# Low parts of the natural weight pieces: formed by accumulating DMAs on GpSimd instead of a subtraction on VectorE

## The reference

```python
S, D = 512, 1024
xn = rms(x, norm_w)                                   # layer 1
h = xn @ w_in                                         # 1024 x 4096
qa, ka, va, ga, qr, kr, vr, gr = split(h)
oa = diff_attention(rms(qa), rms(ka), va, lam)        # 4 heads, two softmaxes each
orr = bidirectional_retention(qr, kr, vr, decays)     # 4 heads, chunks of 128
x = x + concat(rms(oa) * silu(ga), orr * silu(gr)) @ w_out

h = rms_norm(x, norm_g_2)                             # layer 2
v_c, b_c, c_c, z_c, q, k, v, z_a, gates = split(h @ w_in_2)     # 1024 x 8704
y_a = (b_c * causal_conv(c_c * v_c) * silu(z_c)) @ w_conv_out_2
y_b = (sliding_window_attention(rms(q), rms(k), v, sinks) * silu(z_a)) @ w_attn_out_2
g_a, g_b = split(sigmoid(gates + gate_b_2))
out = x + (g_a * y_a + g_b * y_b) @ w_out_2
```

## Time and profile before

| | |
|---|---|
| median of 3 runs | 842.09 us (842.07 to 842.28) |
| profiled execution, its own time | 841.2 us |
| its span in the profile | 839.4 us |
| PE busy | 832.9 us, 3998 matmuls |
| DVE busy | 530.3 us; of it the subtraction L823 158.8 us in 128 |
| ACT busy | 254.9 us |
| POOL busy | 181.1 us; of it the rounding L508 143.9 us in 128 |
| DMA | 74.26 MB, packets 28.9% of 16 engines' span |
| granted clock of PE | 1.00 throughout |

### The profile page before, as it was taken

One profiled execution on the slowest core, in us unless ns is written; L12 is line 12 of the kernel. 1 busy time (PEld: TensorE's weight loads), 2 busy tenths in 40 slices (PEclk: granted clock), 3 DMA queues, 4 the chain that ended last, 5 costly groups with the idle time before them and its releaser, 6 DMA issues.

```text
span 839.4 us, 10665 instructions
## 1 busy us (share of the span) xinstructions
PE 832.9 (99%) x3998; PEld 689.1 (82%) x3998; DVE 530.3 (63%) x1005; ACT 254.9 (30%) x603; POOL 181.1 (22%) x194
## 2 busy tenths in 40 slices
PE   9999999999999999999999999999999999999998
PEld 7787888888888888888888888888888888888886
DVE  4898778868973485785577978796642222444421
ACT  4364465642212234433454455430000000000000
POOL 3121111011111111111223434442211212111210
PEclk9999999999999999999999999999999999999999
DMA  6222211121152322232232222222333333333231
GB/s 234 84 93 85 67 51 51 51 76 51 50 201 76 101 76 76 75 101 76 79 89 80 75 73 75 75 82 80 101 101 101 86 90 101 101 99 90 87 127 73
DMA packets 101225, 74.26 MB, mean 88 GB/s; under 512 B 3325, under 2 KB 87350, under 8 KB 101174
## 3 DMA queue, kind: packets, MB, share of 16 engines
q1 hardware_dynamic: 100614, 71.48, 27.9%
q10 hardware_dynamic: 560, 2.11, 0.7%
HBM read 71.48 MB, written 2.10 MB: 88 GB/s over the span
## 4 chain that ended last, share of the span: by engine, by line
PE 91%; DVE 3%; ACT 2%; SPq 2%; issue 1%; POOL 1%; DMA 1%; ACTq 0%; DVEq 0%; POOLq 0%
PE proj L1231 26%; PE proj L1229 26%; PE proj L1230 26%; PE bank_t L1243 3%; PE bank_o L1315 2%; PE score L1301 1%; PE score L1300 1%; PE score L1390 1%; PE score L1389 1%; DMA w_raw<-in_w_in_dram 1%; PE bank_o L1408 1%; PE score L1277 1%; PE bank_o L1409 1%; ACT mix_hi L703 1%; SPq L453 1%
## 5 line engine op out<-in xcount | busy, mean ns | idle before, releaser
L823 DVE TENSOR_TENSOR w_lo<-w_raw,w_hi 128x1024 fp32r<-128x1024 f32 x128 | 158.8, 1242 | 179.1 <-POOL w_hi L508 178.4
L508 POOL TENSOR_SCALAR w_hi<-w_raw 128x1024 fp32r<-128x1024 f32 x128 | 143.9, 1124 | 552.3 <-DMA w_raw<-in_w_in_dram 389.4
L1229 PE MATMUL proj<-xt_hi,w_hi 128*128 128x512 f32 x512 | 203.0, 397 | 0.0
L1231 PE MATMUL proj<-xt_hi,w_lo 128*128 128x512 f32 x512 | 199.9, 391 | 0.0
L1230 PE MATMUL proj<-xt_lo,w_hi 128*128 128x512 f32 x512 | 199.8, 390 | 0.0
L1231 PEld LDWEIGHTS proj<-xt_hi,w_lo 128*128 128x128 f32 x512 | 96.1, 188 | 20.8
L1230 PEld LDWEIGHTS proj<-xt_lo,w_hi 128*128 128x128 f32 x512 | 96.3, 188 | 19.5
L1229 PEld LDWEIGHTS proj<-xt_hi,w_hi 128*128 128x128 f32 x512 | 96.2, 188 | 19.4
L1229 PE MATMUL proj<-w_hi,yc_hi 128*128 128x512 f32 x160 | 65.1, 407 | 0.0
L1231 PE MATMUL proj<-w_hi,yc_lo 128*128 128x512 f32 x160 | 63.4, 396 | 0.0
L1230 PE MATMUL proj<-w_lo,yc_hi 128*128 128x512 f32 x160 | 63.2, 395 | 0.0
(11 more groups left out here) (280 smaller groups left out, 1352.5 us busy)
## 6 DMA issues: line engine op xcount, KB each, us to landing
w_raw<-in_w_in_dram SPq DMA_DIRECT2D x96, 512.0 KB, 3.7
w_raw<-in_w_out_dram SPq DMA_DIRECT2D x16, 512.0 KB, 3.3
w_raw<-in_w_conv_out_dram SPq DMA_DIRECT2D x8, 512.0 KB, 3.8
w_raw<-in_w_attn_out_dram SPq DMA_DIRECT2D x8, 512.0 KB, 3.8
x_in<-in_x_dram SPq DMA_DIRECT2D x4, 512.0 KB, 8.0
x<-in_x_dram ACTq DMA_DIRECT2D x1, 2048.0 KB, 8.6
out_dram<-x SPq DMA_DIRECT2D x8, 256.0 KB, 3.1
lam_v<-in_lambda_q_dram SPq DMA_DIRECT2D x2, 32.0 KB
```

What stands on the lines that cost most here:

```text
L508: pool.tensor_scalar(w_hi[:, slot, :], w_raw[:, slot, :], 1.0, 1.0, ALU.mult, ALU.mult).then_inc(hi_done, 1)
L823: dve.tensor_tensor(w_lo[:, slot, :], w_raw[:, slot, :], w_hi[:, slot, :].bitcast(F32), ALU.subtract).then_inc(w_split, 1)
L1229: pe.matmul(out, left[0], right[0], start=first, stop=False)
L1231: return pe.matmul(out, left[1], right[0], start=False, stop=last)
```

## The change

For the natural pieces from number 4 on (44 of them: `low_gathered`), the remainder isn't subtracted by DVE any more. POOL, after it has rounded, writes the negated rounded piece over the raw one (`w_lo = w_hi * -1 * 1`), waits until that is done (`minus_done`), and issues a DMA of its own that reads the raw weights from DRAM a second time and adds them to `w_lo` (`accum_op=ALU.add`). PE waits for the landing of that DMA (`low_landed`, one semaphore for each slot) in place of `w_split`. The transposed pieces and pieces 0 to 3 stay with DVE; their count on `w_split` is adapted.

```diff
+def low_gathered(n):
+    return SLOTS <= n and UNIT[n // 4][0] == NAT
+
+def lows_split(n):
+    return sum(not low_gathered(m) for m in range(n + 1))
+
+def lows_gathered(n):
+    return sum(low_gathered(m) and m % SLOTS == n % SLOTS for m in range(n + 1))
...
+        minus_done = sem("minus_done")
+        low_landed = [sem(f"low_landed{i}") for i in range(SLOTS)]
...
+        def natural_source(n):
+            u, q = divmod(n, 4)
+            w, c = UNIT[u][1][0]
+            return a[w][0, 256 * q:256 * q + 256, c:c + 512].rearrange("(k p) c -> p k c", p=P)
...
                 pool.tensor_scalar(w_hi[:, slot, :], w_raw[:, slot, :], 1.0, 1.0, ALU.mult, ALU.mult).then_inc(hi_done, 1)
+                if low_gathered(n):
+                    pool.wait_ge(hi_done, n + 1)
+                    minus = pool.tensor_scalar(w_lo[:, slot, :], w_hi[:, slot, :].bitcast(F32), -1.0, 1.0, ALU.mult, ALU.mult)
+                    minus.then_inc(minus_done, 1)
+                    pool.wait_ge(minus_done, sum(low_gathered(m) for m in range(n + 1)))
+                    pool.dma_start(w_lo[:, slot, :].rearrange("p (k c) -> p k c", k=2), natural_source(n),
+                                   accum_op=ALU.add).then_inc(low_landed[slot], 16)
...
             def split_piece(n):
+                if low_gathered(n):
+                    return
...
+            def wait_low(n):
+                if low_gathered(n):
+                    pe.wait_ge(low_landed[n % SLOTS], 16 * lows_gathered(n))
+                else:
+                    pe.wait_ge(w_split, lows_split(n))
...
                         if e == 0:
-                            pe.wait_ge(w_split, n + 1)
+                            wait_low(n)
...
                     pe.wait_ge(evacuated[q], u)
-                    pe.wait_ge(w_split, n + 1)
+                    wait_low(n)
```

More of the change, by code:

```diff
@@ L445, in load_piece @@
                 if kind == NAT:
-                    w, c = cols[0]
-                    src = a[w][0, 256 * q:256 * q + 256, c:c + 512].rearrange("(k p) c -> p k c", p=P)
+                    src = natural_source(n)
                     dst = w_raw[:, n % SLOTS, :].rearrange("p (k c) -> p k c", k=2)
```

## The result

The kernel with the change took 845.45 us in the median of 4 runs (844.40 to 847.07), the kernel before 842.18 (842.07 to 842.41) beside it: a ratio of 1.0036, 95% interval 1.0024 to 1.0048. It is **slower by some 3 us**, where the prediction had 841.9 and no measurable change. Measured again, as the last experiment, it was 847.65 against 841.93, 1.0073 (1.0055 to 1.0091): the sign is the same, the size differs, and that experiment shows what may make the difference.

A forecast was written before the change was run, and what follows sets the result against it. PE's stream of matmuls was taken as the bound. From the profiled 841.2 us, -0.2 for a wait near the start and 0 for the rest gave 841.0; the median lies 0.9 higher: 841.9 us, range 840.6 to 853.

The forecast's parts named there:

- the reserves of the weight pieces: Time left for an accumulating DMA's issue and landing before PE wants the piece: 9.7 us (piece 32) to 11.8 (piece 4).
- the sum: Profiled 841.2 us, -0.2 for a wait near the start, 0 for subtractions, negations and DMAs: 841.0; median 841.9.
- its cover: The 9.7 to 11.8 us of PE's matmuls that were to hide each piece's negation and DMA.
- full DMA engines: Rival, slower: from 2.5 times a plain load on, transfers pace PE; middle 850 us, chance 0.20.
- late landings: Rival, slower: single accumulations land too late, 1.6 us at piece 4, 3.7 at piece 32; 844 to 847, chance 0.10.
- the idle time of PE after 800 us: Reading of the trace before the change: PE not busy for 3.7 us after 800 us.
- The gain of 0.2 us: Near the start, PE's wait before its matmul at 28.51 goes, as DVE is free 0.56 us earlier: -0.2 us.
- DVE relieved of 54 us: 44 subtractions of 1.23 us leave DVE, some 54 us less busy; nobody waits for them.
- Issue, landing and engine share: Per accumulating DMA: 1 us issue on POOL, 7.9 us landing with company, 2 times a plain load's engine time.
- POOL as the bound: Rival, slower: POOL's issue takes over 3.5 us instead of 1; 858 us at 4.5, chance 0.05.
- the 2.6 us for company: Added to an accumulation's 5.3 us landing for running beside the next piece's load: 7.9 us.
- Slower at all: Chance 0.35 of a measurably slower kernel: full engines 0.20, late single landings 0.10, POOL 0.05.

The follow-up runs named there:

- The halves of the change: The change for natural pieces 4 to 11 only (844.96 us, 1.0036) and for pieces 12 and up only (844.28 us, 1.0026).
- e5_act_negates: The whole change, but ACT makes the negated piece, one piece ahead of its old place; POOL rounds and issues the DMAs: 853.73 us, 1.0136.
- e8_from28: The change for natural pieces 28 and up only, 28 of the 44; earlier ones keep DVE's subtraction: 844.93 us, 1.0024.
- e12_after_again: The whole change once more, nothing altered: 847.65 us, 1.0073 to the kernel before.
- e6_negated_twice: The whole change with each negation made twice in a row on POOL, same result: 853.10 us, 1.0122.

## Why the prediction was wrong

**What bounds the kernel, and the reserves**: PE's stream of matmuls bounded it, and the reserves of the weight pieces were nearly right. The prediction computed them for one kind of work only. "Whatever only prepares the weights costs nothing as long as it comes before PE's turn" left out that POOL's work also slows DVE's, whose chains had 1.04 us in reserve at the keys.

**The failed step** is in the sum: "0 for the subtractions, 0 for negations and DMAs". The negation was priced by its own 1.05 us and its cover on its own chain. Its price is on DVE: 0.7 to 0.8 us for each short operation that meets it, 0.9 us for a product of 128x512 held, on chains that PE waits for; at the keys the result was a wait of 1.6 us where the sum had 0. The sum's other 0, for the DMAs, failed as well: in executions that show it PE waits about 1 us for a low part. The hold was to be seen in the trace of before: an operation of line 809 beside POOL's rounding of piece 5 (POOL, then DVE).

```profile
24.68 1.05 POOL L508 TENSOR_SCALAR w_hi<-w_raw 128x1024 fp32r<-128x1024 f32 x1 [3.14 <-DMA w_raw<-in_w_in_dram]
```

```profile
24.58 0.16 DVE L811 SCALAR_TENSOR_TENSOR rs_y<-rs_t,rs_y 128x4 f32<-128x4 f32 x1
24.78 0.95 DVE L809 SCALAR_TENSOR_TENSOR rs_t<-rs_y 128x4 f32<-128x4 f32 x1
```

0.95 us instead of 0.16, within a stretch that the prediction had read for its 0.2 us; it didn't ask what a second instruction like the rounding would do there. The experiment without DMAs loses 3.0 us, the one with zeros written, 1.0.

**The range** of the prediction, 840.6 to 853, holds both medians, 845.45 and 847.65, but by luck: its upper part was there for full DMA engines and late landings, and the main cause is neither. One reading was off without consequence: the idle time of PE after 800 us is 3.2 us and not 3.7, as the window of the earlier trace rows reaches 0.6 us beyond the end of the span.

**The gain of 0.2 us** came, as far as it can be seen: DVE's `xt_lo` waits for ACT alone, and where zeros were written the matmul of 28.51 stood at 28.53 although its first ones had started 0.2 us later than in the kernel before. In the changed kernel it was more than used up by the second hold of 0.90 us on the same chain.

**DVE relieved of 54 us** was 34.8. The subtractions themselves fell by 158.8 - 104.5 = 54.3 us, as forecast. The remaining 19.5 us are other operations made longer, and overlap with the subtractions that went. Taking every operation of DVE that lasted over 0.3 us more than the shortest of its line and shape, the excess adds up to 24.3 us before and 35.7 after, and every one of them lies beside an instruction of POOL. A DVE that is less relieved than the instructions taken from it was the plainest sign on the page.

**Issue, landing and engine share** were near: 1.24 + 0.30 us for 1.04, 6.5 for 7.9, 2.1 for 2. The rival of full DMA engines is excluded at this factor, with PE unpaced in unit 30 at a share of 0.87, and so is POOL as the bound.

**"Single landings come late"** was the rival that did happen, beside the main cause and not in place of it. Its size was forecast at 1.6 to 3.7 us and is about 1 us in the executions that show it. Its reason was mis-stated: the 2.6 us for company went to the accumulation's own landing, at piece 32; the term left out was the plain load next to it. Piece 31's took 8.5 us instead of 3.5, with x's at 12.8 instead of 8.6, and piece 48's 7.1 instead of 3.7 with no x beside it.

**Slower at all** had a chance of 0.35, all of it on DMA or POOL's time. None of the rivals was the mechanism that decided.

What stays open: the share of each cause. The halves of the change lose 2.8 and 2.1 us, and together 3.3 and 5.7 in two measurements; the place of POOL's instructions against the softmax's chain changes from one execution to the next, and no run here fixed it. The experiments ran on two chips: `e5_act_negates` to `e8_from28` and `e12_after_again` on one, the others on the other (which one the first measurement had isn't known). So the two kernels from piece 28 on, with and without 30 to 33, are compared across chips, each against a median of 842.79 of the kernel before. Nor was x's load tried at another time, nor piece 48's; that its lateness made the wait for `q_stack` is read from the traces and wasn't tested. No version beat the kernel before.

## What to carry to other kernels

- Work moved to GpSimd isn't free because GpSimd has time: look which VectorE operations run beside each of its instructions that read SBUF, and how much reserve the chain they stand in has before TensorE wants its end. Here a reserve of 1.04 us met two holds of 0.75 us and four multiplications drawn out by 1.7. In the softmax one hold was covered, in the kernel before as after; a second, by the negation directly behind the rounding, was not.
- A transfer added beside others is priced three times: its own landing, its share of the engines, and the plain loads next to it. The last was the one that came late, twice.
- Where a kernel's reserves are around 1 us, compare traces only from the first changed instruction on, and take the waits from more than one profiled execution: three kinds of wait took turns here, with medians of 845.45 and 847.65 for the same code.

## What the runs showed of the hardware

The hold is by what POOL does, not by how long: a two-input operation of DVE takes 0.16 us beside a MEMSET of 0.95 us and 0.90 to 0.96 beside a rounding or a negation of 1.05. It works both ways: the rounding that met the product of the keys took 1.40 us instead of 1.05. Where the issue of a DMA on POOL was followed at once by a rounding, a DVE operation of 0.19 us lasted 2.22, to the end of the rounding.

An accumulating DMA of 512 KB lands after 5.5/6.5/8.6 us (shortest, median, longest; plain loads 3.1/3.7/11.0 in the kernel before) and takes 2.1 times a plain load's share of the DMA engines. A plain load of 512 KB issued beside one (piece 31) took up to 8.7 us instead of 3.4, and the 2 MB of x 11.3 to 13.5 us instead of 8.6 to 9.7.

After some of the longer idle times PE's clock fell, and a long wait cost more than its own time. Behind the wait of 4.3 us in `e5_act_negates` (a window; granted clock third from the end) it was at 1.2 GHz, half of the 2.4 GHz of the other stretches:

```profile
252.44:258.40 5.96, 5.96 (x16) 4.69 (x17) 0.00 (x0) 1.06 (x1) 3.30 (x3) 0.50 0.73 158
```

A matmul started every 0.43 us there, against 0.23 at the full clock: 12 products and four transposes (0.36 us where nothing is slow) would have taken 12 x 0.234 + 0.36 = 3.2 of these 5.96 us, so 2.8 us come on top of the wait. In `e6_negated_twice` it fell behind waits of 3.7 and 2.0 us, while behind 1.6 us in the changed kernel and 2.2 us in its second run the starts stood 0.23 apart at once.
